# A second, converting load of every weight unit in place of ScalarE's copy, in a two-layer hybrid decoder trunk

## What is computed

```python
for i in range(DEPTH):                      # 2 layers, D_MODEL 1024, D_FF 2816
    f = swiglu(rmsnorm(h, ffn1_pre_g[i]), ffn1_w_in[i], ffn1_w_down[i])
    h = h + 0.5 * rmsnorm(f, ffn1_post_g[i])
    hn = rmsnorm(h, mix_pre_g[i])
    mixed = gmlp_and_mamba(hn) @ hyb_w_out if i % 2 == 0 else mla_attention(hn, ...)
    h = h + rmsnorm(mixed, mix_post_g[i])
    f = swiglu(rmsnorm(h, ffn2_pre_g[i]), ffn2_w_in[i], ffn2_w_down[i])
    h = h + 0.5 * rmsnorm(f, ffn2_post_g[i])
    gate = jax.nn.sigmoid(rmsnorm(h, ple_pre_g[i]) @ ple_w_gate[i])
    h = h + rmsnorm(gate * (p[i] @ ple_w_proj[i]), ple_post_g[i])
```

## Time and profile before

| what | value |
|---|---|
| median of 2 runs | 1116.66 us (1115.19 to 1118.14) |
| the profiled execution's own time | 1117.32 us |
| its span, first to last instruction | 1115.6 us |
| mean granted TensorE clock | 0.996 |
| PE busy, share of the span | 1103.7 us, 99% |
| PEld | 939.4 us, 84% |
| DVE | 816.3 us, 73% |
| ACT | 565.7 us, 51% |
| POOL | 79.2 us, 7% |
| moved by DMA | 208.37 MB, mean 187 GB/s |

### The profile page before, as it was taken

How to read it: one execution, slowest core, us unless ns; L and a number is a source line. 1 busy time by engine, 2 the same in 40 slices (tenths; PEclk the granted TensorE clock), 3 DMA queues, 4 the chain that set the end, 5 groups by cost and what they waited for, 6 DMA issues and landing times.

```text
span 1115.6 us, 14123 instructions
## 1 busy us (share of the span) xinstructions
PE 1103.7 (99%) x5724; PEld 939.4 (84%) x5724; DVE 816.3 (73%) x1072; ACT 565.7 (51%) x702; POOL 79.2 (7%) x139
## 2 busy tenths in 40 slices
PE   8999999999999999999999999999999999999997
PEld 6888888887888888888888888888898888888886
DVE  5786777578997677677786867768865667676785
ACT  6544444567564554444565544345755555444453
POOL 2200000200110200000013000001100020000011
PEclk9999999999999999999999999999999999999999
DMA  8755554655554565555556555555523365555541
GB/s 309 260 190 189 189 189 163 254 187 176 184 189 151 197 225 190 191 189 189 185 195 219 200 189 189 189 190 173 203 76 114 116 241 187 191 189 193 195 170 57
DMA packets 31600, 208.37 MB, mean 187 GB/s; under 512 B 3760, under 2 KB 3808, under 8 KB 8112
## 3 DMA queue, kind: packets, MB, share of 16 engines
q1 hardware_dynamic: 27936, 194.00, 49.5%
q0 software_dynamic: 3600, 13.46, 3.6%
HBM read 206.39 MB, written 1.06 MB: 186 GB/s over the span
## 4 chain that ended last, share of the span: by engine, by line
PE 95%; DVE 2%; issue 1%; DMA 1%; ACT 1%; POOL 0%; SPq 0%; DVEq 0%; POOLq 0%
PE PS L708 24%; PE PS L186 17%; PE PS L187 17%; PE PS L188 17%; PE PS L711 12%; PE PS L383 1%; PE PS L1928 1%; PE PS L1929 1%; DVE WL L168 1%; PE PS L1226 1%; PE PS L1947 1%; DMA h<-x 1%; PE PS L1937 0%; DMA raw<-stream 0%; ACT WH L161 0%
## 5 line engine op out<-in xcount | busy, mean ns | idle before, releaser
L168 DVE TENSOR_TENSOR WL<-raw,WH 128x2048 fp32r<-128x2048 f32 x180 | 411.3, 2290 | 154.5 <-ACT WH L161 154.1
L161 ACT ACTIVATE WH<-raw 128x2048 fp32r<-128x2048 f32 x180 | 342.8, 1908 | 116.2 <-DMA raw<-stream 116.1
L708 PE MATMUL PS<-X,WH 128*128 128x512 f32 x1152 | 288.4, 392 | 0.0
L708 PEld LDWEIGHTS PS<-X,WH 128*128 128x128 f32 x1152 | 209.1, 189 | 38.9
L711 PEld LDWEIGHTS PS<-X,WL 128*128 128x128 f32 x1152 | 157.2, 190 | 11.3
L711 PE MATMUL PS<-X,WL 128*128 128x256 f32 x1152 | 160.6, 282 | 0.0
L812 ACT ACTIVATE sgb<-sgb 128x256 f32<-128x256 f32 x72 | 30.1, 417 | 228.2 <-DVE sgb L808 228.2
L186 PE MATMUL PS<-WH,X 128*128 128x512 f32 (+3 forms) x360 | 141.5, 393 | 0.5 <-DVE WL L168 0.5
L188 PE MATMUL PS<-WL,X 128*128 128x512 f32 (+3 forms) x360 | 138.8, 385 | 0.0
L187 PE MATMUL PS<-WH,X 128*128 128x512 f32 (+3 forms) x360 | 138.8, 385 | 0.0
L186 PE MATMUL PS<-WH,BH 128*128 128x512 f32 x288 | 113.1, 393 | 0.0
(11 more groups left out here) (282 smaller groups left out, 1306.2 us busy)
## 6 DMA issues: line engine op xcount, KB each, us to landing
raw<-stream SPq DMA_DIRECT2D x181, 1024.0 KB, 4.9
PG<-post_g POOLq DMA_DIRECT2D x8, 512.0 KB, 5.9
QG<-pre_g POOLq DMA_DIRECT2D x7, 512.0 KB, 7.3
raw<-stream SPq DMA_DIRECT2D x4, 512.0 KB, 7.4
Eg<-acs_rows POOLq DMA_DIRECT2D x2, 1024.0 KB, 6.8
h<-x SPq DMA_DIRECT2D x4, 256.0 KB, 6.9
out<-h SPq DMA_DIRECT2D x4, 256.0 KB, 2.0
wsT<-gm_w POOLq DMA_DIRECT2D x1, 512.0 KB, 8.2
```

What stands on the lines that cost most here:

```text
L161: act.activation(WH[:, n % RING, :], raw[:, n % RING, :], ACT.Copy).then_inc(sem("w_hi"), 1)
L168: dve.tensor_tensor(WL[:, n % RING, :], raw[:, n % RING, :], WH[:, n % RING, :], ALU.subtract).then_inc(sem("w_lo"), 1)
L708: pe.matmul(PS[:, bank, :], wh[:, kt, cols], X[:, kt, :, :].rearrange("p a n -> p (a n)"), start=kt == 0, stop=False)
```

## The change

From unit 3 on, the high part no longer comes from ACT. `split_hi` and all its calls are gone. In its place POOL issues a second DMA of the same unit from the stream in HBM, whose destination is `WH` with its rounded type, so the DMA converts on the way. The load for unit n waits for `w_used` as SP's does, and from unit 6 on also for the landing of the high part of unit n-3 (three semaphores `high0` to `high2`). DVE's subtraction waits for both loads. `load_to(n)` stands in POOL's program at chosen places and issues all high loads up to n, so a high load can stand behind POOL's other work. Units 0 to 2 are split as before. Three semaphores of other loads are merged (`hy_gm` and `ml_cg` become `gains_in`).

```diff
@@ loads and splits @@
-        def split_hi(act, n):
+        def load_high(pool, n):
+
             if n >= n_units:
                 return
-            act.wait_ge(sem(f"raw{n % RING}"), 16 * (n // RING + (1 if n % RING > 1 else 0)))
-            act.activation(WH[:, n % RING, :], raw[:, n % RING, :], ACT.Copy).then_inc(sem("w_hi"), 1)
+            if n >= RING:
+                pool.wait_ge(sem("w_used"), n - RING + 1)
+            if n >= 6:
+                pool.wait_ge(sem(f"high{n % 3}"), 16 * (n // 3 - 1))
+            pool.dma_start(WH[:, n % RING, :], a["stream"][n, :, :]).then_inc(sem(f"high{n % 3}"), 16)
 
         def split_lo(dve, n):
 
             if n >= n_units:
                 return
-            dve.wait_ge(sem("w_hi"), n - 2)
+            dve.wait_ge(sem(f"raw{n % RING}"), 16 * (n // RING + (1 if n % RING > 1 else 0)))
+            dve.wait_ge(sem(f"high{n % 3}"), 16 * (n // 3))
             dve.tensor_tensor(WL[:, n % RING, :], raw[:, n % RING, :], WH[:, n % RING, :],
                               ALU.subtract).then_inc(sem("w_lo"), 1)
...
@@ POOL, at a boundary between stages @@
-        def boundary_pool(pool, s):
+        def boundary_pool(pool, s, load_to):
+            m = first[s] if s < NS else n_units
             if s:
+                after_ple = stages[s - 1][0] == "ple"
+                load_to(m + 1 if after_ple else m + 2)
                 post_inverse_rms(pool, s - 1, 0)
+                load_to(m + 3 if after_ple else m + 2)
                 post_inverse_rms(pool, s - 1, 1)
+            load_to(m + 4)
             if s == NS:
                 return
             for t in range(1 if stages[s][0] == "mla" else 2):
...
@@ POOL, in an FFN @@
-        def ffn_pool(pool, s):
+        def ffn_pool(pool, s, load_to):
+            load_to(first[s] + 5)
             if s == 0:
                 prelude_pool(pool)
             if s + 1 < NS and stages[s + 1][0] == "hyb":
-                hyb_early(pool)
+                hyb_early(pool, lambda: load_to(first[s] + 8))
...
@@ POOL, before the masks of the tables, and in the hybrid mixer @@
             pool.dma_start(wsL[:, :, :], a["gm_wl"]).then_inc(sem("hy_ws"), 16)
+            between()
             pool.wait_ge(sem("hy_ws"), 32)
...
+            load_to(u + 16)
             for c in range(2):
                 pool.wait_ge(sem("hy_mv"), c + 1)
...
             rows(0)
 
-            pool.wait_ge(sem("w_used"), first[s] + 18)
+            load_to(u + 22)
+            pool.wait_ge(sem("w_used"), u + 18)
             pool.dma_start(ng[:, :], a["ssd_g"].partition_broadcast(P)).then_inc(sem("hy_ng"), 16)
             pool.wait_ge(sem("hy_yd"), 2)
             rows(1)
             for t in range(2):
+                load_to(u + 23 + 2 * t)
...
@@ the programs of POOL and ACT @@
+            done, load_to = splitter(pool, load_high)
+            done[0] = 3
             for s, (kind, _) in enumerate(stages):
-                boundary_pool(pool, s)
+                boundary_pool(pool, s, load_to)
...
-            done, split_to = splitter(act, split_hi)
-            opening_act(act, done, split_to)
+            opening_act(act)
```

More of the change, by code:

```diff
@@ L440, in load_table, with boundary_act @@
             act.activation(mark[:, 4:5], nhalf[:, 0:1], func)
-        def boundary_act(act, s, split_to):
-            m = first[s] if s < NS else n_units
+        def boundary_act(act, s):
             post_square(act, s - 1, 0)
@@ L511, in first_part_hi, with opening_act @@
             act.activation(part_of(WH, PARTS[i]), part_of(raw, PARTS[i]), ACT.Copy).then_inc(sem("w_part_hi"), 1)
-        def opening_act(act, done, split_to):
+        def opening_act(act):
             act.wait_ge(sem("consts"), 1)
@@ L529, in opening_act @@
             first_part_hi(act, 7)
-            done[0] = 3
         def boundary_dve(dve, s, done, split_to):
@@ L828, in block_low, with ffn_act @@
                .then_inc(sem("b_lo"), 1)
-        def ffn_act(act, s, done, split_to):
+        def ffn_act(act, s):
             f, u = stages[s][1], first[s]
-            after_ple = s > 0 and stages[s - 1][0] == "ple"
-            split_to(u + 3 if s == 0 or after_ple else u + 4)
-            ffn_silu(act, s, f, u + 1, (lambda: split_to(u + 4)) if after_ple else
-                     (lambda: pre_square(act, 0, 1)) if s == 0 else None)
-            split_to(u + 5)
+            ffn_silu(act, s, f, u + 1, (lambda: pre_square(act, 0, 1)) if s == 0 else None)
             rs_row_act(act, f)
-            split_to(u + 6)
             block_silu(act, f, 0)
-            split_to(u + 7)
             ffn_high(act, f)
             block_high(act, f, 0)
-            split_to(u + 8)
             block_silu(act, f, 1)
-            split_to(u + 9)
             block_high(act, f, 1)
-            split_to(u + 10)
             for p in range(8):
-                n, v = u + 8 + 3 * p, 2 + 2 * p
-                last = p == 7
-                split_to(n + 3)
+                v = 2 + 2 * p
                 block_silu(act, f, v)
-                split_to(n + 4)
                 block_high(act, f, v)
                 block_silu(act, f, v + 1)
-                if not last:
-                    split_to(n + 5)
                 block_high(act, f, v + 1)
@@ L1044, in last_dve, with ple_act @@
                 update_h(dve, s, 1, b)
-        def ple_act(act, s, done, split_to):
-            split_to(first[s] + 4)
+        def ple_act(act, s):
             load_table(act, ACT.Sigmoid)
-            split_to(first[s] + 5)
         def ple_dve(dve, s, done, split_to):
@@ L1341, in hyb_pe, with hyb_act @@
                 out_unit(j, t)
-        def hyb_act(act, s, done, split_to):
+        def hyb_act(act, s):
             u = first[s]
@@ L1685, in hyb_dve, with hyb_early @@
             split_to(u + 26)
-        def hyb_early(pool):
+        def hyb_early(pool, between):
             pool.dma_start(dt_w[:, :, :], a["dt_w"]).then_inc(sem("hy_dtw"), 16)
@@ L1702, in hyb_early, with hyb_pool @@
             ins.then_inc(sem("hy_wsm"), 1)
-        def hyb_pool(pool, s):
-            if s == 0:
-                hyb_early(pool)
+        def hyb_pool(pool, s, load_to):
+            u = first[s]
             pool.memset(cx[:, :, 0:3], 0.0).then_inc(sem("hy_pad"), 1)
@@ L2011, in empty, with mla_act @@
             return op(dst, piece_view(n))
-        def mla_act(act, s, done, split_to):
+        def mla_act(act, s):
             u = first[s]
-            split_to(u + 3)
             def latent_squares(t):
@@ L2236, in mla_pool @@
                     inverse_rms(pool, s, 1)
+            load_to(u + 6)
             pool.wait_ge(sem("ml_kr"), 2)
@@ L2249, in mla_pool @@
             ins.then_inc(sem("ml_krr"), 1)
+            load_to(u + 8)
         r_at = s_at + 16384
@@ L2310, in hybrid_trunk @@
         DVES = {"ffn": ffn_dve, "ple": ple_dve, "hyb": hyb_dve, "mla": mla_dve}
-        POOL = {"ffn": ffn_pool, "ple": lambda pool, s: None, "hyb": hyb_pool, "mla": mla_pool}
+        POOL = {"ffn": ffn_pool, "ple": lambda pool, s, load_to: None, "hyb": hyb_pool, "mla": mla_pool}
         block = ctx.enter_context(nc.Block())
```

71 lines of the change are left out of this document (17 added, 54 removed).

## The result

The changed kernel takes **1173.68 us** (median of 2 runs, 1172.84 to 1174.53) against 1116.66 us: a ratio of 1.052, 95% interval 1.0505 to 1.0538. That is 57 us slower. I had forecast 1128 us, 11 us over the kernel before and within 2% of it. The range, 1112 to 1410 us, holds the time, but it is so wide because of a case that did not come true (a slow conversion), so that says little for my working.

A forecast was written before the change was run, and what follows sets the result against it. The prediction took PE to bound the kernel, with the DMA engines close to full. From 1117.3 us it took 1 us for copies and added 3 (start), 5 (units 5 to 8) and 4 (later starts): 1128 us, range 1112 to 1410 us.

The forecast's parts named there:

- a slow conversion: Rival: converting loads hold the 16 DMA engines 4.9 us per unit and set the time; 1400 us, chance 0.23.
- What bounds the kernel, and the steady state: PE sets the time; in the FFNs the DMA engines stay ahead, a pair of loads taking 4.90 of 5.54 us.
- The copies: ACT's 180 removed copies lie beside PE's work; 1 us given back, at most 9.0 us.
- The price of conversion: On the DMA engines a converting load costs the plain price, 2.45 us a unit; far end 4.9 us.
- Both rivals of the rate: On the DMA engines: slower rate, 1140 to 1300 us, chance 0.17; conversion as the bound, 1400 us, chance 0.23.
- The landings: Sign in the changed profile: loads land 6 to 8 us after issue.
- my 223 us: Sign in the changed profile: ACT's busy time falls to about 223 us.
- Start: At the opening, POOL's loads for units 3 and 4 share the engines with the first loads; 3 us (0 to 4.9).
- Units 5 to 8: First FFN: unit 6's high part lands late behind gains and tables, delaying a product PE needs; 5 us (0 to 6).
- Starts of the later stages: At seven later stage starts, gains ahead of the high part make it late for PE; 4 us (0 to 12).
- hybrid mixer 0: In the hybrid mixer, unit 50's high load behind `Eg` lands just in time; no cost, and no slack.
- The one with 0.07: Rival: POOL's program order or descriptor work holds loads back, 5 us at each of eight stages; 1168 us, chance 0.07.

The follow-up runs named there:

- e5: Changed kernel with POOL's first high load delayed until the opening parts landed, and tables, masks and gains spread out among or behind high loads; 1133.19 us.
- e9: Changed kernel with POOL's spread-out order and delayed first high load in the first stage alone; 1158.95 us.
- e2: Changed kernel, but in the first stage alone POOL issues high loads up to unit 8 before gains and tables; 1171.57 us.
- e3: Changed kernel with high loads ahead of the gains in first and later stages, and the first high load waiting for the last opening part; 1149.04 us.
- e8: Changed kernel in its own order, but SP issues unit n's raw load only when unit n-2's high load has landed; 1160.46 us.
- e4: Changed kernel in its own order, with gains PG and QG of only 64 columns from the second stage on; 1156.99 us.
- e7: Changed kernel with its order and waits, but each high load from unit 5 on brings only 64 of 2048 columns; 1142.92 us.
- e10: Kernel of e5, with the gains back in front of the high loads of the sixth to ninth unit in the third FFN alone; 1141.90 us.
- e12: Kernel of e10, with each partition's gain in the third FFN named as four rows of 1 KB; 1143.64 us.
- e13: Kernel before the change, with 146 additional tiny loads issued by POOL in the later two thirds of the four FFNs; 1191.17 us.
- e6: Kernel of e5, with SP issuing unit n's raw load only when unit n-2's high load has landed; 1128.41 us.
- e11: Kernel of e6, with ACT making the high parts of units 96 to 100 by copies as before the change; 1126.98 us.

## Why the prediction was wrong

**What bounds the kernel, and the steady state: right.** PE's period stayed at 16.62 us, the engines' share rose to 1.03 and DVE's subtraction ran ahead of PE. The copies gave back nothing that can be seen.

**The price of conversion: right.** q0 carried 202.22 MB in 44.2% of the engines' time, q1 194.00 MB in 45.0%: a converted megabyte costs no more than a plain one. Both rivals of the rate fall. In windows of a settled FFN the engines moved 398 to 424 GB/s. The Trainium skill's rule (HBM Reference, Specifications: about 358 GB/s per core) is passed here; its own exception for a core that streams alone is what the trace shows. The landings, 6.0 and 8.3 us, lie about where I put them. ACT's 243.6 us are 20 us over my 223 us.

**Start: in bounds.** 3 us forecast (0 to 4.9), 4.6 us measured at matmul 64. e5 and e9, which delay the first high load until the opening parts are there, are 2.4 to 2.6 us ahead at that place. The bounds are as narrow as the spread between traces, so the hit is in part luck.

**Units 5 to 8: a term that was mis-sized.** 5 us forecast (0 to 6), 13.4 us measured. The mechanism is the one I named: unit 6's high part behind gains and tables, and the product behind the subtraction. Three sizes were off. POOL issued the gains at 31.1 us and not at 25.4 us, 5.7 us later, of which 4.6 us are the late start that PE shares. From there unit 6 took 23.9 us to land (55.0 us); I had 15.0 to 20.8 us. In that time q1 moved 3.34 MB beside it where I had put 2.1 MB, and both queues together 8.34 MB, 350 GB/s. Those two make 4.2 us more than my upper end. The last 3.0 us are the clock after the stall, for which I had no term. A second wait stands behind the first: POOL masks the tables when they have landed, and unit 9's high load waits for POOL. In the changed kernel it is hidden; e2 and e3 uncover it, and e9 takes both away down to 4.5 us between matmul 64 and matmul 300.

**Starts of the later stages: the term that failed most.** 4 us forecast for seven starts (0 to 12), hybrid mixer 0. Measured: 6.4 + 2.8 + 7.6 + 12.1 + 6.8 = 35.7 us, the hybrid mixer's among them. Of the 6.4 us in that column 5.5 lie at the mixer's start; nearly 2 more come about 330 us, where DVE has waited 1.74 us for unit 50 behind `Eg`, the place that I had put at no cost (some 0.8 us in between are won back). The step that failed is "1.05 MB of gains stand ahead of the high part (2.45 us) and its own 2.45 us replace ACT's 1.9". It prices the queue as if q0 had the engines to itself. It does not: in the same microseconds PE frees four places of the ring and SP issues four raw loads (633.1 to 641.3 us). Unit 102's high load, from issue to landing, measures it: 15.6 us in the changed kernel, 11.7 us with the raw loads paced (e8), 12.6 us with small gains (e4), 11.2 us with 32 KB in place of 1 MB (e7), 8.3 us with the gains behind it (e5), and 15.9 us with them in front again (e10). Each of the raw loads beside it, the gains' bytes and its own bytes is worth 3.0 to 4.4 us of its landing; having no gains ahead at all is worth 7.3 us. The Trainium skill states how the engines serve queues (DMA: Bandwidth & Descriptors, Queues, rings and completion order): each takes turns between them, a packet at a time. The landings here agree with that in kind; how the turns divide the bytes I have not shown, since e12 did not change the packets. And "other boundaries look alike" was not read from them: the losses go from 2.2 us at the second FFN's start, the one I had read, to 12.1 us at the third's.

**The tail: no term.** 3.4 us of 57, tied by e13 to POOL's added DMAs, whatever they carry.

**The rivals.** The one with 0.07, POOL's program order at 5 us for each of eight stages, 1168 us, was the right mechanism in its first half, and nearly the right time. e5 takes 41 us away with the same bytes, e10 puts 9 us back. Its time is near by luck: the sum is one of unequal stages, 18.0 us in one and nothing in others, and not by eight times 5 us. It said that DMA would be idle beside PE's waits; the windows show 332 to 430 GB/s there, because the late load competes with early ones. Its second half, descriptor work held back by DVE, is not seen: POOL's 180 issues took 537 ns each beside DVE's subtractions. I set it low because one issue takes 0.55 us, which speaks of its length and not of its place.

**Shares of the 57 us.** Order of POOL's program and the delayed first load: 41 us (e5), up to 7 of them the delay. Pacing of the raw loads: 5 us more (e6). Tail: about 3 us. The rest, some 9 us by the medians and 5 us by the profiled executions, lies mostly at the boundary behind the ple and is not told apart further. One rival stands untested: the change also makes POOL wait for the landing of the high load three units back, 57.7 us in all and at most 11.3 us at once, with everything behind it on POOL waiting too. No run leaves that wait out. No version beats the kernel before, and by the sum none can by much: the copies that were removed had cost PE at most 9 us. The best, e11 and e6, are 1.0% and 1.2% slower.

## What to carry to other kernels

When a transfer is moved to another engine's queue, ask what stands in front of it there at every stage boundary (waits, tables, gains), and who stands behind the instruction that will wait for it. A late load in an in-order program starves work that does not need it. Price a queue that shares full engines by what the other queue is doing in those microseconds, not by the engines' whole rate; and where one wait is lifted, name the next one on the same queue before counting the gain.

## What the runs showed of the hardware

- A load that converts f32 to fp32r on the way moved at the same rate as a plain one (44.2% of the engines' time for 202.22 MB, 45.0% for 194.00 MB).
- A PE stall of 10.4 us took the granted clock to 0.50, and it was still 0.50 at 64 us, 5 us after PE had resumed. The place lost 13.4 us.
- Each kernel with 146 to 180 additional DMAs by POOL, tiny ones too, ended 2.9 to 3.8 us later behind its last matmul, with nothing recorded there.
- A load of 32 KB on q0 landed after 2.3 us with no other load in flight, and after 11.2 us behind 1 MB of gains and beside four loads of 1 MB on q1 (e7).
